# First RMSNorm of a hybrid decoder step: input laid out by channel on the host, sum of squares by a product with ones

## What is computed

```
def rmsnorm(x, w):
    xf = x.astype(jnp.float32)
    y = xf * lax.rsqrt(jnp.mean(xf * xf, axis=-1, keepdims=True) + EPS)
    return (y * w.astype(jnp.float32)).astype(x.dtype)

z = rmsnorm(x, norm1_w) @ w_in          # w_in: 1024 x 5632
```

## Time and profile before

| | |
|---|---|
| median of 3 runs | 1768.83 us |
| the profiled execution: its time | 1766.95 us |
| its span in the trace | 1765.1 us |
| TensorE matmul busy | 1553.6 us (88%) |
| VectorE busy | 707.0 us (40%) |
| ScalarE busy | 461.4 us (26%) |
| GpSimd busy | 232.3 us (13%) |
| DMA | 186.03 MB, mean 105 GB/s |

### The profile page before, as it was taken

How to read it: one execution, slowest core, us unless ns; L and a number is a source line. 1 busy time by engine, 2 the same in 40 slices (tenths; PEclk the granted TensorE clock), 3 DMA queues, 4 the chain that set the end, 5 groups by cost and what they waited for, 6 DMA issues and landing times. The chain is left out here.

```text
span 1765.1 us, 22053 instructions
## 1 busy us (share of the span) xinstructions
PE 1553.6 (88%) x7497; PEld 1061.8 (60%) x7498; DVE 707.0 (40%) x1465; ACT 461.4 (26%) x1040; POOL 232.3 (13%) x417
## 2 busy tenths in 40 slices
PE   5999889977499899898879999999889937999996
PEld 3555556555356565555558888888768733444442
DVE  4356877666524444454542221233242251212220
ACT  2223333322123333333432121122132210111110
POOL 1000101010122221222210000000000001222221
PEclk8999999988789998999979999999989968999998
DMA  7000300000030202000034766523253383988973
GB/s 246 16 1 17 116 2 26 1 2 25 26 114 1 62 1 62 1 26 1 1 121 135 249 205 204 168 72 110 84 158 108 108 288 105 317 247 231 297 215 48
DMA packets 119369, 186.03 MB, mean 105 GB/s; under 512 B 9507, under 2 KB 82262, under 8 KB 117222
## 3 DMA queue, kind: packets, MB, share of 16 engines
q1 hardware_dynamic: 107750, 134.41, 24.0%
q0 software_dynamic: 11520, 50.34, 9.8%
HBM read 154.38 MB, written 30.34 MB: 105 GB/s over the span
## 5 line engine op out<-in xcount | busy, mean ns | idle before, releaser
L964 PE MATMUL psum<-attention_part,kept 128*128 128x384 f32 (+1 forms) x576 | 201.0, 504 | 0.8 <-DVE attention_part L1197 0.7
L2158 PE MATMUL psum<-moe_part,kept 128*128 x384 | 172.4, 603 | 6.4 <-issue 4.9
L964 PEld LDWEIGHTS psum<-attention_part,kept 128*128 128x128 f32 (+1 forms) x576 | 108.0, 192 | 76.1 <-issue 16.5
L1430 PE MATMUL psum<-split 128*128 128x368 f32 x384 | 140.6, 366 | 2.5 <-DVE split L1576 2.5
L498 PE MATMUL psum<-kept,recurrence_part 128*128 128x368 f32 x384 | 124.4, 480 | 10.0 <-PEq L236 5.0
L1419 PE MATMUL psum<-kept,sample_part 128*128 128x368 f32 x384 | 131.8, 487 | 1.3 <-PEq L865 1.3
L503 PE MATMUL psum<-recurrence_part,kept 128*128 128x512 f32 (+1 forms) x288 | 126.5, 594 | 1.3 <-DVE kept L684 1.3
L1432 PE MATMUL psum<-split 128*128 128x368 f32 x384 | 127.3, 332 | 0.0
L1431 PE MATMUL psum<-split 128*128 128x368 f32 x384 | 127.0, 331 | 0.0
L2158 PEld LDWEIGHTS psum<-moe_part,kept 128*128 128x128 f32 x384 | 72.3, 193 | 89.7 <-issue 89.7
L518 PE MATMUL psum<-recurrence_part 128*128 128x128 f32 (+1 forms) x480 | 70.8, 308 | 48.9 <-DVE recurrence_part L767 39.4
(11 more groups left out here) (312 smaller groups left out, 2519.6 us busy)
## 6 DMA issues: line engine op xcount, KB each, us to landing
sample_part<-merge_gates POOLq DMA_DIRECT2D x16, 1024.0 KB
merge_part<-cache_kT SPq DMA_DIRECT2D x64, 256.0 KB, 3.3
merge_part<-cache_v SPq DMA_DIRECT2D x64, 256.0 KB, 3.0
moe_part<-w_gate SPq DMA_DIRECT2D x16, 1024.0 KB, 6.1
moe_part<-w_up SPq DMA_DIRECT2D x16, 1024.0 KB, 12.5
moe_part<-w_down SPq DMA_DIRECT2D x16, 1024.0 KB, 14.1
recurrence_part<-w_in SPq DMA_DIRECT2D x8, 1024.0 KB, 8.2
sample_part<-merge_out POOLq DMA_DIRECT2D x16, 512.0 KB, 6.5
```

The source lines that it names most:

```text
L964: mm = pe.matmul(bank_of(("z", h, i))[:ROWS[i], 0:384], K["xT"][:, k, cols(i)], Wb[h % 2][:, k, :], start=(k == 0), stop=(k == KC - 1))
L1430: pe.matmul(bank_of(u, 2 * j + 1), wh[w % 2][:, k, ch], xh[b][:, k, :], start=(k == 0), stop=False)
L2158: mm = pe.matmul(psum[:, 2 + par, :], XT[par][:, k, :], K["GU"][:, bass.ds(KC * b + k, 1), :], start=(k == 0), stop=(k == KC - 1))
```

## The change

The host now makes one array `xT`: the 1104 token rows in six parts of 184, each with channels on partitions (128 x 8 x 184 f32). It also lays out the small vectors as one 128 x 19 array. SyncE requests the vectors and all six parts at once, each part into a buffer of its own, then the first block of recurrence weights, then the small inputs (`ident` among them, which the phase no longer uses), then the second block. For each part ScalarE squares all 1472 columns into one of two buffers; TensorE adds the squares over channels by eight accumulated matmuls of 184 columns with a 128x128 matrix of ones, so that every partition of PSUM holds the sum of each token; VectorE scales that and adds EPS (184 columns); GpSimd raises it to the power -0.5 for all 184 columns; VectorE writes `xT` with eight scalar_tensor_tensor instructions of 184 columns (x times norm weight times the power). The transposes, the row-wise scaling and the wide PSUM evacuation are gone.

```diff
+XN = 6
+XC = TOK // XN
...
+        xin, sq = [sb(KC, XC) for _ in range(XN)], [sb(KC, XC) for _ in range(2)]
+        mean, rstd, power, ones = sb(XN, XC), sb(XN, XC), sb(XC), sb(P)
...
         @block.sync
         def _(sp):
+            sp.dma_start(vec, A["vectors"]).then_inc(vec_in, 16)
+            for i in range(XN):
+                sp.dma_start(xin[i].rearrange("p a b -> p (a b)"), A["xT"][i]).then_inc(x_in[i], 16)
+            load_recurrence_block(sp, A, K, 0)
             sp.dma_start(K["ident"], A["ident"]).then_inc(const_in, 16)
...
-            load_recurrence_block(sp, A, K, 0)
             load_recurrence_block(sp, A, K, 1)
...
         @block.scalar
+            for i in range(XN):
+                act.wait_ge(x_in[i], 16)
+                if i >= 2:
+                    act.wait_ge(summed, i - 1)
+                act.activation(sq[i % 2], xin[i], ACT.Square).then_inc(squared, 1)
...
         @block.gpsimd
+            pool.memset(ones, 1.0).then_inc(setup, 1)
             pool.memset(power, -0.5).then_inc(setup, 1)
             pool.memset(K["half"], -0.5).then_inc(setup, 1)
+            pool.wait_ge(setup, 3)
+            for i in range(XN):
+                pool.wait_ge(mean_done, i + 1)
+                pool.tensor_tensor(rstd[:, i, :], mean[:, i, :], power, ALU.pow).then_inc(rstd_done, 1)
...
         @block.vector
+            def average(i):
+                dve.wait_ge(summed, i + 1)
+                dve.tensor_scalar(mean[:, i, :], psum[:, i, 0:XC], 1.0 / D, EPS, ALU.mult, ALU.add).then_inc(mean_done, 1)
+
+            def scale(i):
                 dve.wait_ge(rstd_done, i + 1)
+                for k in range(KC):
+                    dve.scalar_tensor_tensor(K["xT"][:, k, part(i)], xin[i][:, k, :], vec[:, k:k + 1], rstd[:, i, :], ALU.mult, ALU.mult)
+
+            dve.wait_ge(vec_in, 16)
+            for i in range(XN):
+                average(i)
+                if i:
+                    scale(i - 1)
+            scale(XN - 1)
...
         @block.tensor
+            pe.wait_ge(setup, 1)
+            for i in range(XN):
+                pe.wait_ge(squared, i + 1)
                 for k in range(KC):
+                    mm = pe.matmul(psum[:, i, 0:XC], ones, sq[i % 2][:, k, :], start=(k == 0), stop=(k == KC - 1))
+                mm.then_inc(summed, 1)
...
+    x = np.concatenate([arrays["meta_tokens"], arrays["x_sample"].reshape(NSAMP, D), arrays["x_prompt"][0]])
+    arrays["xT"] = x.reshape(XN, XC, KC, P).transpose(0, 3, 2, 1).reshape(XN, P, KC * XC).copy()
```

More of the change, by code:

```diff
@@ L238, in phase_norm1 @@
         sem = lambda n: nc.alloc_semaphore(name="norm1_" + n)
[L239 to L245, removed]
+        vec_in, const_in, setup = sem("vec_in"), sem("const_in"), sem("setup")
+        x_in = [sem(f"x_in{i}") for i in range(XN)]
+        squared, summed, mean_done, rstd_done = sem("squared"), sem("summed"), sem("mean_done"), sem("rstd_done")
+        lb_max, lb_exp, lam_dot, lam_exp = sem("lb_max"), sem("lb_exp"), sem("lam_dot"), sem("lam_exp")
+        xin, sq = [sb(KC, XC) for _ in range(XN)], [sb(KC, XC) for _ in range(2)]
+        mean, rstd, power, ones = sb(XN, XC), sb(XN, XC), sb(XC), sb(P)
         lp, lpp, dots, lm = sb(4, 64), sb(2, 64), sb(2), sb(3, HEADS)
         vec = K["vecT"]
+        part = lambda i: slice(XC * i, XC * i + XC)
         block = st.enter_context(nc.Block())
@@ L271, in _ @@
             sp.dma_start(K["table"][0:1, :], A["page_table"].rearrange("a b -> (a b)").unsqueeze(0)).then_inc(const_in, 16)
-            load_recurrence_block(sp, A, K, 0)
             load_recurrence_block(sp, A, K, 1)
             sp.wait_ge(const_in, 80)
-        def x_ready(e, i):
-            e.wait_ge(x_in[i % 3], 32 if i == 0 else 16 * (i // 3 + (2 if i % 3 == 0 else 1)))
         @block.scalar
         def _(act):
[L281 to L286, removed]
+            for i in range(XN):
[3 more added lines that the diff above has]
+                act.activation(sq[i % 2], xin[i], ACT.Square).then_inc(squared, 1)
             act.wait_ge(lb_max, 1)
@@ L312, in _ @@
-            for i in range(NT):
-                r = ROWS[i]
-                x_ready(dve, i)
-                dve.wait_ge(rstd_done, i + 1)
[L316 to L324, removed]
@@ L325, in _ @@
-            evacuate(NT - 1)
+            def average(i):
+                dve.wait_ge(summed, i + 1)
+                dve.tensor_scalar(mean[:, i, :], psum[:, i, 0:XC], 1.0 / D, EPS, ALU.mult, ALU.add).then_inc(mean_done, 1)
+            def scale(i):
+                dve.wait_ge(rstd_done, i + 1)
+                for k in range(KC):
+                    dve.scalar_tensor_tensor(K["xT"][:, k, part(i)], xin[i][:, k, :], vec[:, k:k + 1], rstd[:, i, :], ALU.mult, ALU.mult)
+            dve.wait_ge(vec_in, 16)
@@ L356, in _ @@
         def _(pe):
[L357 to L364, removed]
+            pe.wait_ge(setup, 1)
+            for i in range(XN):
+                pe.wait_ge(squared, i + 1)
                 for k in range(KC):
-                    mm = pe.transpose(psum[:, 2 * (i % 2) + k // 4, P * (k % 4):P * (k % 4) + r],
-                                      xn[:r, i % 2, P * k:P * k + P], K["ident"][:r, :r])
-                mm.then_inc(turned, 1)
+                    mm = pe.matmul(psum[:, i, 0:XC], ones, sq[i % 2][:, k, :], start=(k == 0), stop=(k == KC - 1))
+                mm.then_inc(summed, 1)
 def phase_recurrence(nc, A, K, out, sb, psum):
@@ L2283 @@
     arrays["merge_gates"] = np.stack(branch_gate, axis=3).transpose(2, 1, 0, 3, 4).reshape(KC, P, -1).copy()
+    x = np.concatenate([arrays["meta_tokens"], arrays["x_sample"].reshape(NSAMP, D), arrays["x_prompt"][0]])
+    arrays["xT"] = x.reshape(XN, XC, KC, P).transpose(0, 3, 2, 1).reshape(XN, P, KC * XC).copy()
+    rows = [arrays.pop("norm1_w").reshape(KC, P), arrays.pop("hg_lb_logits").reshape(2 * HEADS, P), arrays.pop("hg_onorm_w"),
+            arrays.pop("da_onorm_w"), np.tile(arrays.pop("q_norm_w"), (1, 2))]
+    arrays["vectors"] = np.concatenate(rows).T.copy()
     arrays.update(constants())
```

## The result

The changed kernel takes 1928.43 us (median of 4 runs, 1926.86 to 1936.46) against 1769.17: ratio 1.0902, 95% interval 1.0873 to 1.0931. It is 9% slower, some 159 us. The forecast was 1930. It is so near by luck: two of its terms were wrong by almost the same amount with opposite signs, which the following rows show.

What follows compares the result with a forecast made beforehand. It took the end of norm1 as fully on the path, bound by six GpSimd powers: 32.7 us plus six times 27.7 put the first product at 198.9 instead of 35.83 us; 1766.95 + 163 = 1930 us, range 1903 to 1950.

Steps and rivals of the forecast that it cites:

- powers back to back with scaling beside them: Sign in norm1 that would show the forecast wrong: GpSimd's powers follow without gaps while VectorE scales beside them.
- rival B: Norm1: power cost linear in columns, but VectorE isn't held up; phase 185.3 us, +149.5, total 1916; chance 0.11.
- linear power with exclusion: Main case in norm1: power cost grows with columns and powers exclude VectorE's scaling; +163 us, total 1930; chance 0.73.
- GpSimd's price per column: Norm1's power: cost goes with the columns, some 0.4 us fixed; 184 columns take 27.7 us, bounds 0.9 and 30.7.
- rival C: Norm1's power: slope falls with width, say to 74 ns; power 14.3 us, phase 118.5, +83, total 1850; chance 0.05.
- The hold of VectorE: Norm1: VectorE's two-operand scaling cannot run beside a GpSimd power; one excludes the other for a whole instruction.
- the written order: VectorE in norm1: average(2) stands behind scale(0), and so on, so each later power's period is 30.5 us.
- The start of the row and the tail: Norm1's ends: first power at about 12.9 us; after the last, scaling 2.4, `lb` and `lam` chain 3.0, barrier 0.8.
- Rival A: Norm1: wide power is cheap (0.9 us), TensorE the bound; phase ends at 31.9 us, -3.9, total 1763; chance 0.07.
- about 1.5 us: Norm1: price of one wide power above which the cheap-power case no longer gains time.
- The loads and the rest: Recurrence weights land by about 20 and 27 us, so reordered requests cost nothing; everything behind norm1 is unchanged.
- One microsecond more or less: End of norm1: fully on the path, so each microsecond there is one of the span, if what follows is unchanged.

## Why the forecast held, step by step

The price of the power was right in kind, and it carries nearly all of the 160 us. That the total came within 2 us is luck: the mechanism forecast between the powers did not occur. Two of the forecast's own signs say so. The first VectorE instruction of a group was to last as long as a power and lasted 0.73 us; "powers back to back with scaling beside them", the sign of rival B, is what the trace shows. B had been given 0.11, linear power with exclusion 0.73.

**GpSimd's price per column: right in kind, 7% low.** The step "at 184 columns the last slope gives 27.7 us" measured 29.74; the slope of wide powers is 160 ns, between the two that the forecast had (148 and 165). Six times 2.0 is +12 us. That the cost goes with the columns decided sign and size, and rival C is excluded (14.3 us a power).

**The hold of VectorE: wrong.** "These cannot run beside a power", and from it the written order with 2.8 us between the powers from power 2 on. The rows it rested on were multiplications on one side (rows 12, 13) and a VectorE instruction that came first on the other (rows 10, 11). Neither showed how long a power holds VectorE, and the forecast took the whole instruction. Measured: 0.34 us of 29.74. So powers run back to back: the part of the phase that isn't power is 197.71 - 178.35 = 19.4 us, not 32.7, that is -13 us. Together with the +12 the error is 1.2 us in 198.9. Rival B was right on this point, and with the true price its sum is 12.9 + 178.4 + 6.2 = 197.5. On the contention the Trainium skill (page "SBUF — State Buffer", section "SBUF: two separate sides") says the shared port pair is held for the full instruction; here a GpSimd power held VectorE for about 1% of its time and the multiplication of 1152 columns for nearly all of it. The measurement decides: for the power the rule does not hold.

**The start of the row and the tail: right.** First power at 12.44 (12.9 forecast), first sums 4.2 us (4.95 forecast, all at the low clock; they sped up at 10.5 us) and the second part's 2.4; last scaling 2.65 (2.4), chain 3.5 (3.0), barrier 0.8.

**Rival A: priced wrongly, though it did not come up.** It took TensorE as the bound behind a cheap power and gave -3.9 us. Without the power the phase was 2.4 us longer than before, since VectorE's own work, eight narrow instructions and an average, is 3.16 us a part. The step that failed added one part's scaling behind the last sum instead of comparing the sums over six parts of each engine. The forecast's own terms would have shown it: 2.4 for a scaling and 0.4 for an average are 2.8 us a part on VectorE, against 2.5 on TensorE. Its "about 1.5 us", above which the gain is gone, has no working. So with a power as cheap as a multiplication the phase was still no shorter than before. It became shorter only when VectorE's work was cut and the power moved to ScalarE.

**The loads and the rest: right.** They landed far ahead, and the stages behind kept their length in sum to 2 us in 1727. "One microsecond more or less" holds for a loss only: the run with the constants early in the kernel before met the weight load after 1 us of gain.

## What to carry to other kernels

When an operation moves from one number per partition to a row on every partition, read its price per column from the same operation at two or three widths; the instruction count fell here from nine to six while the columns raised went from 9 to 1104. Then add up each engine's work per part, not only the one that looks busy: behind the first bound stood VectorE, and behind an early barrier stood a weight load. A hold seen with one kind of instruction does not carry over to another by its duration; here it went with the operand columns. And before a price is read from a trace, see at which clock it was paid: the distance between equal records tells it where the clock column does not.

## What the runs showed of the hardware

A GpSimd power costs 0.3 us and 160 ns a column from 138 to 368 columns; VectorE's reciprocal costs 1.30 us at 184 columns, where a scalar_tensor_tensor costs 0.40. ScalarE's inverse root of 184 columns from PSUM takes 0.41 us. GpSimd stretches a VectorE instruction with two SBUF operands by 0.22, 0.34 and 0.72 us beside powers of 138, 184 and 368 columns that last 22, 30 and 59 us, and by 0.33 beside a multiplication of 184 columns that lasts 0.67. The granted clock is listed as 1.00 from the start of each trace, but the first part's sums took 4.2 us and the next 2.4. The first matmul records begin 0.307 us apart and those from 10.5 us on 0.156, so the first ran at 1.2 GHz. With weight loads back to back and matmuls of one column TensorE ran at 1.2 GHz through all six parts, 0.153 us for a load of 92 columns.
